# First layer's feed-forward: both streams in one matmul per weight tile, 512 moving columns instead of twice 256

## The reference, cut to what matters

```python
def swiglu(h, w_in, w_out):
    gu = jnp.einsum('bld,de->ble', h, w_in)          # 1024 -> 2 x 2816
    g, u = jnp.split(gu, 2, axis=-1)
    return jnp.einsum('blf,fd->bld', jax.nn.silu(g) * u, w_out)   # 2816 -> 1024

# layer l, main stream x and context stream xc
x = x + g2 * swiglu(modulate(rms_norm(x, norm2_g[l]), sh2, sc2), w_ffn_in[l], w_ffn_out[l])
if not last:
    xc = xc + cg2 * swiglu(modulate(rms_norm(xc, norm2_g[l]), csh2, csc2),
                           w_ffn_in[l], w_ffn_out[l])
```

## Time and profile before

| | |
|---|---|
| Time, median of 3 runs | 1656.06 us (1655.53 to 1656.3) |
| Profiled execution, first to last instruction | 1652.8 us |
| What lies around the span (median less span) | 3.3 us |
| PE busy | 1595.9 us, 97% |
| PE weight load busy | 1465.8 us, 89% |
| DVE busy | 1120.9 us, 68% |
| ACT busy | 921.6 us, 56% |
| Read from device memory | 298 MB, 181 GB/s |

### The profile page before, as it was taken

The page is one execution under the profiler, slowest core; times in us unless marked ns, Lnnn a source line. Parts: engine busy times, 40 slices in busy tenths (PEclk is TensorE's granted clock), DMA queues, the critical chain, the costliest instruction groups (busy, mean ns, idle before and its releaser), DMA issues. The chain is left out here.

```text
span 1652.8 us, 31090 instructions
## 1 busy us (share of the span) xinstructions
PE 1595.9 (97%) x12890; PEld 1465.8 (89%) x12890; DVE 1120.9 (68%) x1763; ACT 921.6 (56%) x1467; POOL 132.4 (8%) x106
## 2 busy tenths in 40 slices
PE   5999989999999999989999999999999999999999
PEld 2987578999999999966899999878999998799999
DVE  2799667645566655897754556777887567788873
ACT  3444656645365444647554445766666467676662
POOL 0230000112001100300012100000011000001110
PEclk8999999999999999999999999999999999999999
DMA  9433666656546555435466553314555633235553
GB/s 386 161 147 142 255 230 232 228 223 233 194 167 222 200 187 200 154 128 217 172 216 201 187 198 130 117 56 144 194 200 187 216 118 118 78 132 203 206 190 120
DMA packets 45164, 301.09 MB, mean 182 GB/s; under 512 B 5232, under 2 KB 7504, under 8 KB 11744
## 3 DMA queue, kind: packets, MB, share of 16 engines
q1 hardware_dynamic: 44304, 297.44, 50.6%
q0 software_dynamic: 288, 0.92, 0.1%
q10 hardware_dynamic: 432, 0.75, 0.1%
HBM read 298.02 MB, written 1.06 MB: 181 GB/s over the span
## 5 line engine op out<-in xcount | busy, mean ns | idle before, releaser
L2018 DVE TENSOR_TENSOR wl<-raw,wh 128x1040 fp32r<-128x1040 f32 (+1 forms) x472 | 567.3, 1241 | 313.1 <-ACT wh L1771 220.6
L1771 ACT ACTIVATE wh<-raw 128x1040 fp32r<-128x1040 f32 (+1 forms) x472 | 465.5, 1030 | 182.7 <-PE bank L1560 95.2
L1555 PE MATMUL bank<-hx_hi,wh 128*128 128x256 f32 x1856 | 522.6, 282 | 6.0 <-ACT hx_hi L1771 3.8
L1560 PE MATMUL bank<-hx_lo,wh 128*128 128x256 f32 x1856 | 516.7, 278 | 0.0
L1558 PE MATMUL bank<-hx_hi,wl 128*128 128x256 f32 x1856 | 514.6, 277 | 0.2 <-DVE wl L2018 0.2
L1555 PEld LDWEIGHTS bank<-hx_hi,wh 128*128 128x128 f32 x1856 | 349.1, 188 | 12.8 <-issue 11.8
L1558 PEld LDWEIGHTS bank<-hx_hi,wl 128*128 128x128 f32 x1856 | 349.0, 188 | 4.3 <-issue 3.6
L1560 PEld LDWEIGHTS bank<-hx_lo,wh 128*128 128x128 f32 x1856 | 348.9, 188 | 1.2 <-DVE hx_lo L2011 0.4
L1558 PE MATMUL bank<-hid_hi,wl 128*128 128x256 f32 x912 | 252.2, 277 | 1.1 <-DVE wl L2018 1.1
L1555 PE MATMUL bank<-hid_hi,wh 128*128 128x256 f32 x912 | 252.4, 277 | 0.1
L1560 PE MATMUL bank<-hid_lo,wh 128*128 128x256 f32 x912 | 252.0, 276 | 0.0
(11 more groups left out here) (219 smaller groups left out, 1909.1 us busy)
## 6 DMA issues: line engine op xcount, KB each, us to landing
raw<-in_wts SPq DMA_DIRECT2D x208, 1032.0 KB, 4.9
raw<-in_wts SPq DMA_DIRECT2D x50, 1024.0 KB, 6.5
raw<-in_wts SPq DMA_DIRECT2D x20, 776.0 KB, 4.2
raw<-in_wts SPq DMA_DIRECT2D x4, 584.0 KB, 4.2
tmp<-tscr SPq DMA_DIRECT2D x16, 128.0 KB, 3.9
raw<-in_wts SPq DMA_DIRECT2D x2, 648.0 KB, 3.9
xTc<-in_ctxT SPq DMA_DIRECT2D x1, 1024.0 KB, 10.8
xTx<-in_xT SPq DMA_DIRECT2D x1, 1024.0 KB, 8.1
```

What stands on the lines that cost most here:

```text
L1555: pe.matmul(out, block(f, M.wh, w0 + k, ncols, c, m), x_hi, start=first and k == 0 and o == 0, stop=False, skip_group_check=True)
L1560: ins = pe.matmul(out, block(f, M.wh, w0 + k, ncols, c, m), x_lo, start=False, stop=last and k == nk - 1, skip_group_check=True)
L1771: return act.activation(out, in_, func, bias=bias, scale=scale)
L2018: tt(M.wl[k][:, cols], M.raw[r][:, cols], M.wh[k][:, cols].bitcast(F32), ALU.subtract).then_inc(*on.inc(lo))
```

## The change

The first feed-forward is rewritten as `ffn_both`.

- **Layout.** The high parts of x's and c's input lie in one tensor (`h_hi`, stream x and then stream c), likewise the low parts (`h_lo`). `H["xc"]` is a view of both streams for one k. In the profile and the order both streams' inputs are now called `h_hi` and `h_lo`, everywhere in the program.
- **Up product.** Step 0 is still done for each stream alone (`first_pair`): half of c's gate gemm, then the root of x's norm, the other half, c's second gemm, and only then x's two gemms with the same two weight pieces. Steps 1 to 10 use `gemm_both`: the moving operand is 512 columns (256 of x, 256 of c), an output tile fills a whole bank, and the piece is used once.
- **Inner blocks.** The hidden tiles are kept for 8 tiles and both streams (`hid8`) and written over in turn. After up steps 0 to 3, and again after steps 4 to 7, the part of the down product over these 8 tiles is done for both streams at once, and added to x and c by the new step `resid2`.
- **Last part.** After steps 8 to 10 the down product over the last 6 tiles is done for c, four groups of 36 matmuls of 256 columns, and then for x, with the same four pieces taken a second time. The norms of the next layer are built there; that of c is started after x's first group.

In numbers: of the 3168 matmuls of 256 columns 2688 become 1344 of 512 columns, and 480 stay (192 in `first_pair`, 288 in the last part). 30 pieces are no longer read and split (22 up, 8 down).

```diff
@@ Memory
-            self.H[s] = (sb(f"h{s}_hi", [P, 8, T], F32R), sb(f"h{s}_lo", [P, 8, T], F32R))
+        h = sb("h_hi", [P, 2, 8, T], F32R), sb("h_lo", [P, 2, 8, T], F32R)
+        self.H = {s: tuple(v[:, i] for v in h) for i, s in enumerate("xc")}
+        self.H["xc"] = tuple(v[:, :].rearrange("p s k t -> p k s t") for v in h)
...
+        both = rh("hid8_hi", [P, 8, 2, T], F32R), rh("hid8_lo", [P, 8, 2, T], F32R)
+        self.hid8 = {s: tuple(v[:, :, i] for v in both) for i, s in enumerate("xc")}
+        self.hid8["xc"] = tuple(v[:, :] for v in both)
@@ Plan
+    def gemm_both(self, f, a, a_toks, nk=8, first=True, last=True):
+        f = self.take(f)
+        tiles = [(P * j, P, 0, self.banks.get()) for j in range(2)]
+        return [b for _, _, _, b in tiles], self.gemm(f, nk, 256, tiles, a, a_toks, first=first, last=last)
@@ plan_program, ffn_both
+        def first_pair():
+            fg = take(("up1", 0, 0), look=False)
+            bg_ = banks.get()
+            tiles = [(0, P, 0, bg_), (P, P, T, bg_)]
+            p.gemm(fg, 4, 256, tiles, H["c"], ht["c"], last=False, done=False)
+            norm_x.root()
+            tg = p.gemm(fg, 4, 256, tiles, H["c"], ht["c"], k0=4, w0=4, first=False, done=False)
+            up = gate("c", bg_, tg)
+            step("log_set")
+            fu = take(("up1", 0, 1))
+            finish_ffn_in("x")
+            bu, tu = p.gemm_pair(fu, H["c"], ht["c"], done=False)
+            parts = {"c": up(bu, tu, [h[:, 0:2, :] for h in M.hid8["c"]])}
+            bg_, tg = p.gemm_pair(fg, H["x"], ht["x"])
...
+        def pair(i):
+            at = 2 * i % 8
+            bs, tg = p.gemm_both(("up1", 0, 2 * i), H["xc"], both)
+            ups = [gate("xc", b, tg) for b in bs]
+            split_late()
...
+            bs, tu = p.gemm_both(("up1", 0, 2 * i + 1), H["xc"], both)
...
+        for kb in range(3):
+            for i in (range(4), range(4, 8), range(8, 11))[kb]:
+                mod_fill(i % 2, (1, 2, 0))
...
+            split_late()
+            if kb < 2:
...
+                for ch in range(4):
+                    bs, tk = p.gemm_both(("dn1", 0, ch, kb), M.hid8["xc"], toks8)
+                    add_both(ch, bs, tk)
...
+        for s in "cx":
+            nrm = Norm(s)
+            for ch in range(4):
...
+                f = take(("dn1", 0, ch, 2))
+                if ch == 3:
+                    tk = [p.gemm(f, 6, 256, tiles[j:j + 1], M.hid8[s], tiles_of[s], done=j == 1) for j in range(2)]
+                else:
+                    tk = [p.gemm(f, 6, 256, tiles, M.hid8[s], tiles_of[s])] * 2
+                ts = add_resid(s, tiles, tk, ch, mvec(0, s, 5), t_mod[(0, 2)], ready[s][2 * ch:2 * ch + 2])
+                nrm.add(ch, ts, single=ch == 3)
+                if s == "x" and ch == 0:
+                    behind.pop()()
+            region_free[:] = [tk[1]]
+            with_norm(s, nrm, ts[1])
...
-    for s in "cx":
-        hd = ffn1(0, s, ht[s], ffn_step)
-        nn, t = ffn_down("dn1", 0, s, hd, mvec(0, s, 5), t_mod[(0, 2)], [], True)
-        behind.append(lambda s=s, nn=nn, t=t: finish_layer(s, nn, t))
+    ffn_both(norm["x"], lambda s, nn, t: behind.append(lambda: finish_layer(s, nn, t)))
@@ tensor_program, gemm
-            x_hi, x_lo = a[0][:, k0 + k, :], a[1][:, k0 + k, :]
+            x_hi, x_lo = a[0][:, k0 + k], a[1][:, k0 + k]
-                out = b.t[0:m, o:o + T]
+                out = b.t[0:m, o:o + T] if len(x_hi.shape) == 2 else b.t[0:m, :].rearrange("p (s t) -> p s t", s=2)
@@ vector_program
+    def resid2(c, b, tk, gates, ready, ts):
+        on.wait_ge(tk, ready)
+        for j, s in enumerate("xc"):
+            stt(M.xT[s][:, c, :], b.t[:, j * T:j * T + T], gates[j][:, c:c + 1], M.xT[s][:, c, :], ALU.mult,
```

More of the change, by code:

```diff
@@ L192, in __init__ @@
         self.xT["c"] = sb("xTc", [P, 8, T])
-        self.H = {}
-        for s in "xc":
-            align(0)
-            self.H[s] = (sb(f"h{s}_hi", [P, 8, T], F32R), sb(f"h{s}_lo", [P, 8, T], F32R))
+        align(0)
+        h = sb("h_hi", [P, 2, 8, T], F32R), sb("h_lo", [P, 2, 8, T], F32R)
+        self.H = {s: tuple(v[:, i] for v in h) for i, s in enumerate("xc")}
+        self.H["xc"] = tuple(v[:, :].rearrange("p s k t -> p k s t") for v in h)
         self.raw = [sb(f"raw{i}", [P, SLOT]) for i in range(NRAW)]
@@ L239, in __init__ @@
         self.hid = (rh("hid_hi", [P, FT, T], F32R), rh("hid_lo", [P, FT, T], F32R))
+        rh = area(reg_off)
+        both = rh("hid8_hi", [P, 8, 2, T], F32R), rh("hid8_lo", [P, 8, 2, T], F32R)
+        self.hid8 = {s: tuple(v[:, :, i] for v in both) for i, s in enumerate("xc")}
+        self.hid8["xc"] = tuple(v[:, :] for v in both)
         rb = area(b1_off)
@@ L988, in parts @@
                 t = (ev("hid_hi"), ev("hid_lo"))
-                step("hidsplit", i=i, y=y, ready=m, t=t,
+                step("hidsplit", out=[h[:, 2 * i:2 * i + 2, :] for h in M.hid], y=y, ready=m, t=t,
                      free=flat([region_free, kv_free, q_free["x"], q_free["c"], pc_free["x"], pc_free["c"]]))
@@ L1908, in silu, with hidsplit @@
         fn(sl.t[:, :], b.t[:, :], ACT.Silu).then_inc(*on.inc(t))
-    def hidsplit(i, y, ready, free, t, **_):
+    def hidsplit(out, y, ready, free, t):
         on.wait_ge(ready, free)
-        o = M.hid[0][:, 2 * i:2 * i + 2, :].rearrange("p a t -> p (a t)")
-        fn(o, y.t[:, :], ACT.Copy).then_inc(*on.inc(t[0]))
+        fn(out[0], y.t[:, :].rearrange("p (a t) -> p a t", a=2), ACT.Copy).then_inc(*on.inc(t[0]))
     def lambdas(lsum, t_s, t_e, **_):
@@ L2164, in resid @@
                 ALU.add).then_inc(*on.inc(ts[j]))
+    def resid2(c, b, tk, gates, ready, ts):
+        on.wait_ge(tk, ready)
+        for j, s in enumerate("xc"):
+            stt(M.xT[s][:, c, :], b.t[:, j * T:j * T + T], gates[j][:, c:c + 1], M.xT[s][:, c, :], ALU.mult,
+                ALU.add).then_inc(*on.inc(ts[j]))
     def gate1(sl, a, b, tk, y, free, t, **_):
@@ L2288, in vector_program @@
                 "conv1": conv1, "conv2": conv2, "exp1": exp1, "wt1": wt1, "sub1": sub1, "pcsplit": pcsplit,
-                "stsplit": stsplit, "resid": resid, "gate1": gate1, "lambdas": lambdas, "tables": tables,
+                "stsplit": stsplit, "resid": resid, "resid2": resid2, "gate1": gate1, "lambdas": lambdas, "tables": tables,
                 "lora2": lora2, "mla_k2": mla_k2, "exp2": exp2, "wt2": wt2, "val2": val2, "tconv": tconv,
@@ L2318, in pools, with hidsplit @@
                 tt(dst[:, :, 0:n], src[:, :, 0:n], src[:, :, sh:sh + n], ALU.add).then_inc(*on.inc(ts[3 * g + 3]))
-    def hidsplit(i, y, free, t, **_):
-        hi, lo = (h[:, 2 * i:2 * i + 2, :].rearrange("p a t -> p (a t)") for h in M.hid)
+    def hidsplit(out, y, free, t, **_):
         on.wait_ge(t[0], free)
-        tt(lo, y.t[:, :], hi.bitcast(F32), ALU.subtract).then_inc(*on.inc(t[1]))
+        tt(out[1], y.t[:, :].rearrange("p (a t) -> p a t", a=2), out[0].bitcast(F32),
+           ALU.subtract).then_inc(*on.inc(t[1]))
     def gate2(i, yu, t, free, **_):
```

59 lines of the change are left out of this document (added).

## The result

The changed kernel takes 1672.3 us (1671.0 to 1673.0, 4 runs), the kernel before 1655.8 on the same chip (1654.7 to 1656.3, 4 runs): a ratio of 1.0103, interval 1.0088 to 1.0117, or +16.5 us. The forecast was 1664.3, +8.2. The profiled execution has a span of 1670.4, before 1652.8.

A forecast was written before the change was run, and what follows sets the result against it. PE was taken to bound the kernel, never idle in the first feed-forward. Stream -0.7, start +3.8, entry +1.0, end +4.1 made +8.2 on span 1652.8: 1661.0, plus 3.3 for the median, 1664.3 us; 8-in-10 range 1648 to 1671.

The forecast's parts named there:

- the stream term: First feed-forward: 1344 matmuls of 512 columns at 226.5 ns replace 2688 of 256 at 113.5 ns, -0.7 us.
- the end: From c's last group to the next layer's start: PE waits for late splits and sums, +4.1 us, between 2 and 6.
- the entry: Start of the last part: PE waits for the second hidden tile's low part, 0.6 to 2.2 us, taken as +1.0.
- rival 4: Stream over two separate blocks of h_hi and h_lo takes 232.5 ns per matmul: +7.4 us, time 1672, chance 0.08.
- grows with the columns: Feed-forward matmuls: the 6.8 ns over the clock at 256 columns rise with width, second 256 columns costing 113 ns; chance 0.50.
- the question that the forecast put, matmul or columns: Whether the 6.8 ns over the clock at 256 columns belong to each matmul or to its columns; the gain rests on it.
- Rivals 2 and 3: Stream spacing: 2, extra per matmul, 220.1 ns, 1655.7 us, chance 0.22; 3, no extra, 213.3 ns, 1646.6 us, chance 0.13.
- The rule of the Trainium skill: Stream: columns at 2.4 GHz plus some 2.5 ns, 215.8 ns at 512 columns; would give 290.0 us, 15 us less.
- Start: Feed-forward start: PE loses 1.8 us at x's root and 2.0 in x's first gemm, together +3.8 us.
- the root's wait: Next layer's start: x's root waits 2.5 us for the folded sum, after PE has ended 48 matmuls.
- the split of x's last piece: End of the feed-forward: its low half is ready at 14.7, PE wants it at 13.5, 1.2 us lost.
- 30 fewer splits: Feed-forward: pieces no longer split on ACT and DVE, about 31 MB not read, counted zero behind a PE that doesn't wait.

The follow-up runs named there:

- experiment 1: Kernel of matmuls alone, operands resident, shapes and offsets varied: 512 columns took 233.3 ns with weights 64 bytes into a 128-byte line, 226.2 with them on it.
- experiment 5: Matmuls alone again, 20 phases with offsets, predecessors and one- or two-block sources varied: 512 columns took 227.0 ns at equal offsets, 233.3 at 64 bytes apart.
- experiments 8 and 9: 8: matmuls alone, high and low weights' offsets varied apart, 227.0 to 233.3 ns at 512 columns. 9: changed kernel with equal offsets within 256 bytes, 1665.4 us.
- experiment 3: Changed kernel with its first two hidden steps run per stream, c then x, weight pieces loaded and split twice: 1668.3 us.
- Experiment 4: Changed kernel with hidden steps 8 to 10 and their down product run per stream, c then x, pieces loaded and split twice: 1664.5 us.
- experiment 2: Changed kernel with each joint 512-column matmul issued as two of 256, same buffers, splits and waits: 1666.8 us.

## Why the prediction was wrong

The step that failed is the stream term: "I take 113.5 + 113 = 226.5 ns, 304.4 us in all: -0.7 us." It measured 231.9 ns and +6.6. The terms together came to 18.0 us where 8.2 were forecast. Of these 9.8 us 7.3 sit here; the end took 3.0 more than its term and the entry 0.55 less. The 113 came out of 389 - 276, and the 389 was called "512 columns 389 ns at best"; the other five figures in the earlier trace rows (the least, the median and the largest of two groups of eight) were 395 to 400. I took the least of six figures for the mean of 1344. From their mean of 395 come 395 - 276 = 119 and 232.5 ns, the number that I put at the high end and gave 0.08 as rival 4. Rival 4's result was nearly right (+6.6 against its +7.4; 1672 against 1672.3), its reason was not: two separate blocks are not slower than one (experiments 1 and 5). I also used a start-to-start reading of seven matmuls, 228 ns, as support. The trace of before has 24 of them, in two groups of twelve. The second, from the same line in a later layer, starts and ends with

```profile
1387.34 0.40 PE L1583 MATMUL bank<-wh,ckn_hi 128*128 128x512 f32 x1
...
1389.91 0.40 PE L1583 MATMUL bank<-wh,ckn_lo 128*128 128x512 f32 x1
```

which is 234 ns for each, against 229 to 230 in the first. The 22 spacings of both groups have a mean of 231.7: the price was on record, and the seven were the fast part of it.

226.5 is, to 0.2 ns, the matmul at equal offsets (experiments 8 and 9). That is luck: nothing in the working knew of offsets, and the price belongs to a layout that this kernel doesn't have.

That the extra "belongs to fp32r's full-rate stream and [...] grows with the columns" was right only in part. In the kernel's own layout the extra over the clock goes from 6.7 ns at 256 columns to 18.5 at 512, nearly three times. At equal offsets it doesn't grow: 120.0, 173.4 and 226.7 ns at 256, 384 and 512 columns are 13.3 or 13.4 over the clock each time, with 448 columns (206.6, 19.9 over) apart. The row of the 384, from experiment 5:

```profile
L94 PE MATMUL bank<-hi,wh x48: 334/334/339, 413.6 to 438.0; 128*128 128x384 f32 x48
```

So the extra isn't a matter of columns alone, and neither half of the question that the forecast put, matmul or columns, had the layout in it. Rivals 2 and 3 would have shown 220 and 213 to 216; no fp32r layout had these, only bf16 came to 216.1. The rule of the Trainium skill (TensorE: Matmul & The Clock Gate, Back-to-back issue gap), columns at 2.4 GHz and some 2.5 ns, gives 215.8: this case bears it out for bf16 at 512 columns (216.1) and not for fp32r, at 256 or 512.

The waits. Start: +3.8 forecast, +3.8 in the trace, and experiment 3 gave back 4.0 by median, of which 0.5 was to come from fewer 512-column matmuls. At the root this is luck in part: the forecast let it start at once and wait for the last square, and in the trace it waited at its start, for DVE's fold, and met the square without a wait; both end it at the same time. Entry: +1.0 taken, +0.45, because POOL's two low parts took 1.30 each, the lower of the two lengths in the earlier trace rows. End: the root's wait was forecast at 2.5 and was 2.4 (2.6 with the slower start behind it); the split of x's last piece cost 2.3 in place of 1.2; the clock's fall, 1.7, was not in the forecast at all. The split came late because c's norm did. Its first scaling stands 7.7 us behind the end of c's last group (642.4), where the forecast had 6.5:

```profile
648.59 0.63 ACT L1886 ACTIVATE tmp<-xTx 128x512 f32<-128x512 f32 x1 [2.09 <-DVE xTx L2125]
...
650.07 0.88 DVE L2125 SCALAR_TENSOR_TENSOR tmp<-xTc,amod,tmp 128x256 f32<-128x256 f32 x2 [1.57 <-ACT tmp L1886]
```

c's root ended at 647.55, but on ACT's queue the squares of x's first group stand ahead of the logarithm, and they waited for DVE's addition. The forecast counted 1.35 us from the root to the scaling, as if ACT were free. Experiment 4 gave back 7.9 by median, expected 7.5 to 8. The range of 1648 to 1671 was made to stop short of rival 4, and the measured 1672.3 is where that rival, with its 0.08, lay.

That 30 fewer splits and 31.7 MB less traffic count zero was right: experiment 2 has them too, and its 256-column matmuls run at the pace of before, 353 in 40 us against 354.

## To carry to other kernels

A spacing is the mean over a whole repeating pattern, start to start, never the best duration; where six figures disagree by 3%, the term's sum must be made from their mean and the range from both ends, and all groups of such rows must be read, not the first. For fp32r matmuls, look at where weights and moving operand lie within 256 bytes, for each of the alternating weight buffers, and measure it for the width in use: the layout that is best for 256 columns is a bad one for 512. Work that was taken out from beside a busy engine was worth nothing here, while the cover that went with it cost time at both ends.

## What was not expected of the hardware

- The spacing of an fp32r matmul depends on the addresses of weights against moving operand, with a period of 256 bytes: 226.7 to 234.2 ns for 512 columns, 113.3 to 120.0 for 256. Low weights alone out of line are enough (231). What inside the engine does this is not shown.
- The best layout of 512 columns is the worst of those tried for 256: equal offsets give 226.7 and 120.0. The kernel's own, high weights 64 and low 192 bytes off, has 113.3 for 256, the least found (both 192 bytes off, and high 192 with low 64, have it too), and 231.9 at 512.
- At equal offsets the time over the clock was 13.3 to 13.4 ns at 256, 384 and 512 columns. 128 columns, with both weights 64 bytes off, took 111.3 ns (experiment 1), nearly as much as 256 columns, so a narrower matmul brought next to nothing there.
- With 256 columns and both weights 64 bytes off, one and the same loop ran at 117.8 in most phases and at 113.3 in others. What moves it from one to the other stays open.
- After a wait of 1 to 2.4 us at the end of the feed-forward the granted clock fell to half for some 3 us, in each of the five kernels with the joint end, which cost 1.7 us in the changed one; in the four with split ends, where PE had no such wait, it stayed at 1.00 there.
